# Samples' value products with probabilities stationary, and their last chain inside the cz tiles

## What is computed

```python
o_cmp, p_cmp = cmp_attention(q, pos, kc, vc)                # 63 compressed keys
o_slc = slc_attention(q_rot, pos, idx, ks_blk, vs_blk)      # 1024 cached keys + the new one
o_win = win_attention_cached(q_rot, pos, ...)               # window of 512
g3 = jax.nn.sigmoid(cg).reshape(B, T, 3, C_HEADS, 1)
oc = g3[:, :, 0] * o_cmp + g3[:, :, 1] * o_slc + g3[:, :, 2] * o_win
yc = oc.reshape(B, T, C_WIDTH).astype(x.dtype) * jax.nn.silu(cz)
```

## Time and profile before

| what | us |
|---|---|
| median of 3 runs (lowest to highest) | 1960.08 (1957.07 to 1964.10) |
| the profiled execution | 1959.96 |
| its span | 1958.2 |
| TensorE matmuls busy | 1695.2 (87%) |
| DVE, ACT, POOL busy | 955.0, 560.5, 481.6 |
| mean granted TensorE clock | 0.918 |

### The profile page before, as it was taken

One profiled execution on the slowest core, in us unless ns is written; L12 is line 12 of the kernel. 1 busy time (PEld: TensorE's weight loads), 2 busy tenths in 40 slices (PEclk: granted clock), 3 DMA queues, 4 the chain that ended last, 5 costly groups with the idle time before them and its releaser, 6 DMA issues. The chain is left out here.

```text
span 1958.2 us, 30111 instructions
## 1 busy us (share of the span) xinstructions
PE 1695.2 (87%) x11721; PEld 1503.9 (77%) x11721; DVE 955.0 (49%) x1621; ACT 560.5 (29%) x1111; POOL 481.6 (25%) x468
## 2 busy tenths in 40 slices
PE   7899978988886999999896996978778996999797
PEld 3789965666665888888796986878677985899797
DVE  0651466666640222422212394858454265568676
ACT  0312125444431232332110342434232355100100
POOL 2022101000011111111202472737363212124400
PEclk9999959999988999999897997979789997999899
DMA  8401140000005444343303110202021201344422
GB/s 297 139 11 45 23 99 1 1 2 2 1 21 146 117 114 109 103 112 100 134 22 120 33 33 11 68 15 63 11 88 55 60 23 45 139 143 141 153 77 76
DMA packets 166720, 144.47 MB, mean 74 GB/s; under 512 B 55254, under 2 KB 156594, under 8 KB 165682
## 3 DMA queue, kind: packets, MB, share of 16 engines
q1 hardware_dynamic: 157586, 128.80, 22.0%
q10 hardware_dynamic: 8992, 13.74, 2.0%
HBM read 117.32 MB, written 29.40 MB: 75 GB/s over the span
## 5 line engine op out<-in xcount | busy, mean ns | idle before, releaser
L1008 PE MATMUL ps<-w_hi,h_hi 128*128 128x256 f32 x792 | 229.8, 290 | 19.1 <-DVE h_lo L2462 13.6
L1008 PE MATMUL ps<-h_hi,w_hi 128*128 128x344 f32 x648 | 222.8, 344 | 10.0 <-DVE aq L2301 5.1
L1008 PE MATMUL ps<-w_lo,h_hi 128*128 128x256 f32 x792 | 225.4, 285 | 0.0
L1008 PE MATMUL ps<-w_hi,h_lo 128*128 128x256 f32 x792 | 225.3, 284 | 0.0
L1008 PE MATMUL ps<-h_lo,w_hi 128*128 128x344 f32 x648 | 216.2, 334 | 0.0
L1008 PE MATMUL ps<-h_hi,w_lo 128*128 128x344 f32 x648 | 215.2, 332 | 0.0
L1008 PEld LDWEIGHTS ps<-w_hi,h_hi 128*128 128x128 f32 x792 | 152.7, 193 | 20.2 <-issue 14.5
L1008 PE MATMUL ps<-h_hi,wg_hi 128*128 128x344 f32 x432 | 148.5, 344 | 14.9 <-ACT gate_stage L1752 13.7
L890 POOL CAST w_hi<-w_raw 128x1024 fp32r<-128x1024 f32 (+1 forms) x50 | 53.7, 1074 | 419.2 <-DMA w_raw<-in_w_in 186.6
L1008 PEld LDWEIGHTS ps<-w_lo,h_hi 128*128 128x128 f32 x792 | 152.7, 193 | 0.0
L1008 PEld LDWEIGHTS ps<-w_hi,h_lo 128*128 128x128 f32 x792 | 152.6, 193 | 0.0
(11 more groups left out here) (434 smaller groups left out, 3620.6 us busy)
## 6 DMA issues: line engine op xcount, KB each, us to landing
w_raw<-in_w_in SPq DMA_DIRECT2D x46, 512.0 KB, 5.1
sgm<-gate_spill SPq DMA_DIRECT2D x22, 516.0 KB, 5.7
gate_spill<-gate_stage ACTq DMA_DIRECT2D x54, 172.0 KB, 2.5
w_raw<-in_w_in SPq DMA_DIRECT2D x34, 256.0 KB, 3.4
adw<-in_ada_w SPq DMA_DIRECT2D x8, 1024.0 KB, 11.2
pgc<-in_cache_nsa_kv SPq DMA_DIRECT2D x128, 64.0 KB, 2.4
pg<-in_cache_nsa_kv SPq DMA_DIRECT2D x64, 128.0 KB
w_raw<-in_w_branch SPq DMA_DIRECT2D x12, 512.0 KB, 4.5
```

Of the source, the lines that this page charges most:

```text
L1008: last = mm(out, lhsT=l, rhs=r, start=(i == 0 and j == 0), stop=(i == n - 1 and j == 2))
```

## The change

The value products exchange their operands: 8 columns of `PTS` are stationary and 128 columns of values move, so that the outputs come as 8 rows (heads) x 384. DVE copies them to the dead rows of `CS` or `CSR` (`OT8`), and SP places each sample's 8 rows by a DMA in rows `8b` to `8b + 7` of a new tile `OROW` (`o_rows`), for samples 0 to 5 in front of the value loads of the sample two later, for sample 6 behind the last sample's loads, and for sample 7 behind the loads of cz's weights. DVE waits for the placement before it writes the same buffer again. The transposes of `OTS` (L1407) and `OTS` itself are gone. The spreading of the cz and gate rows stands behind tile 4 of cz, DVE's chain behind tile 5 (with ACT's two sigmoids), and the turning back behind tile 7; the copy into `YF` and `yc_done` stay behind the last tile.

```diff
@@ -405,12 +405,13 @@
     QBD = sb("qbd", o_, [2, 64]); o_ += 128
     NKT = sb("nkt", o_, [8]); o_ += 8
     PTS = sb("pts", o_, [112]); o_ += 112
-    OTS = sb("ots", o_, [3, 64]); o_ += 192
     SM8 = sb("sm8", o_, [16], parts=8); o_ += 16
     assert o_ <= END
     o_ = O_F + 14864
     PW8 = sb("pw8", o_, [512], parts=8); o_ += 512
     NVR = sb("nvr", o_, [2, P], parts=1); o_ += 256
+    OROW = sb("o_rows", o_, [3, P], parts=64); o_ += 384
+    OT8 = [CS[:, 0:384], CSR[:, 0:384]]
     assert o_ <= O_F + 16128
     EXQ = sb("exq", O_SRW, [512], parts=64)
     QROW = sb("qrow", O_SRW + 512, [2, P], parts=64)
@@ -505,6 +506,7 @@
     gate_full, gate_free = sem("gate_full"), sem("gate_free")
     gate_out = [sem("gate_out%d" % i) for i in range(2)]
     spilled = sem("spilled")
+    o_placed, placed_before = [ld["x2"], adw_in[3]], 5 * 16
     half_split = sem("half_split")
     w_used = sem("w_used")
     own = {n: sem("own_" + n) for n in ("act", "dve", "pool")}
@@ -714,6 +716,12 @@
         sp.wait_ge(outs, total[0])
         cache = a["cache_nsa_kv"][0].rearrange("n p f g d -> n p (f g d)")
         npool = cache.shape[0]
+
+        def place_output(b):
+
+            sp.wait_ge(e("s_ots"), b + 1)
+            sp.dma_start(OROW[8 * b:8 * b + 8].rearrange("q x c -> q (x c)"), OT8[b % 2]).then_inc(o_placed[b % 2], 16)
+
         for b in range(NS):
             def page(j):
                 i = sp.value_load(KP[0:1, 8 * b + j:8 * b + j + 1], min_val=0, max_val=npool - 1)
@@ -736,6 +744,7 @@
             load_more_gate_weights(2 * b + 3 + (b >= 3))
             if b >= 2:
                 sp.wait_ge(e("s_pv"), b - 1)
+                place_output(b - 2)
             for j in range(8):
                 sp.dma_start(PG[:, b % 2, j, :], page(j).rearrange("o p c -> p (o c)")[:, 256:512]).then_inc(pg_in[b % 2], 16)
             wv = swin[b].rearrange("(t p) c -> p t c", p=P)
@@ -743,11 +752,13 @@
             sp.dma_start(WR[:, b % 2, 1:4, :], wv[:, 1:4, :]).then_inc(pg_in[b % 2], 16)
             sp.dma_start(WR[0:1, b % 2, 0, :], CS[b:b + 1, 1024:1280]).then_inc(pg_in[b % 2], 16)
             sp.dma_start(NVR[:, b % 2, :], CS[b:b + 1, 896:1024]).then_inc(pg_in[b % 2], 16)
+        place_output(NS - 2)
         load_more_gate_weights(len(SGATES))
         sp.wait_ge(half_split, halves_plain + len(SGATES))
         half[0] += len(SGATES)
         for u in range(U_CZ, U_A):
             load_unit(u)
+        place_output(NS - 1)
         for b in range(NS):
             out_dma(win_s[b, 0:511, :], swin[b, 1:512, :])
         load_unit(U_A)
@@ -1362,12 +1373,12 @@
             nc.tensor.transpose(ps[:, 6, 0:8], PW8[:, 384:512], ID[0:8, 0:8]).then_inc(e("s_pt"), 1)
             gates(b, 8)
             pe.wait_ge(e("s_pts"), b + 1)
-            mm(ps[:, 6, 8:16], lhsT=VCS[0:NCMP, :], rhs=PTS[0:NCMP, 0:8], start=True, stop=True)
+            mm(ps[0:8, 6, 0:P], lhsT=PTS[0:NCMP, 0:8], rhs=VCS[0:NCMP, :], start=True, stop=True)
             for i in range(8):
-                mm(ps[:, 6, 16:24], lhsT=PG[:, s, i, P:2 * P], rhs=PTS[:, 8 + 8 * i:16 + 8 * i], start=(i == 0), stop=False)
-            mm(ps[:, 6, 16:24], lhsT=NVR[:, s, :], rhs=PTS[0:1, 72:80], start=False, stop=True)
+                mm(ps[0:8, 6, P:2 * P], lhsT=PTS[:, 8 + 8 * i:16 + 8 * i], rhs=PG[:, s, i, P:2 * P], start=(i == 0), stop=False)
+            mm(ps[0:8, 6, P:2 * P], lhsT=PTS[0:1, 72:80], rhs=NVR[:, s, :], start=False, stop=True)
             for i in range(4):
-                last = mm(ps[:, 6, 24:32], lhsT=WR[:, s, i, P:2 * P], rhs=PTS[:, 80 + 8 * i:88 + 8 * i], start=(i == 0), stop=(i == 3))
+                last = mm(ps[0:8, 6, 2 * P:3 * P], lhsT=PTS[:, 80 + 8 * i:88 + 8 * i], rhs=WR[:, s, i, P:2 * P], start=(i == 0), stop=(i == 3))
             last.then_inc(e("s_pv"), 1)
             gates(b, 9)
         pe.wait_ge(e("s_ots"), NS)
@@ -1396,20 +1407,19 @@
             last.then_inc(pz.full, 1)
             if t >= 2:
                 yc_transposes(pe, t - 1)
+            if t == 4:
+                pe.wait_ge(e("cs_cz"), 1)
+                mm(ps[0:64, 6, 0:512], lhsT=G[0:8, GE8:GE8 + 64], rhs=CS[:, 1304:1816], start=True, stop=True)
+                mm(ps[0:64, 7, 0:24], lhsT=G[0:8, GE8:GE8 + 64], rhs=CS[:, 1280:1304], start=True, stop=True).then_inc(e("f_psum"), 1)
+            if t == 7:
+                pe.wait_ge(e("f_sbuf"), 2)
+                for i in range(4):
+                    last = mm(ps[:, 7, 416 + 8 * i:424 + 8 * i], lhsT=YSM[:, P * i:P * i + P], rhs=G[0:64, GE64:GE64 + 8], start=True, stop=True)
+                last.then_inc(e("f_psum"), 1)
         pe.wait_ge(pz.full, 9)
         pe.sem_inc(w_used, 2)
         yc_transposes(pe, 8)
 
-        pe.wait_ge(e("cs_cz"), 1)
-        mm(ps[0:64, 6, 0:512], lhsT=G[0:8, GE8:GE8 + 64], rhs=CS[:, 1304:1816], start=True, stop=True)
-        mm(ps[0:64, 7, 0:24], lhsT=G[0:8, GE8:GE8 + 64], rhs=CS[:, 1280:1304], start=True, stop=True)
-        for i in range(3):
-            last = nc.tensor.transpose(ps[0:64, 7, 32 + P * i:32 + P * i + P], OTS[:, i, :], ID)
-        last.then_inc(e("f_psum"), 1)
-        pe.wait_ge(e("f_sbuf"), 2)
-        for i in range(4):
-            last = mm(ps[:, 7, 416 + 8 * i:424 + 8 * i], lhsT=YSM[:, P * i:P * i + P], rhs=G[0:64, GE64:GE64 + 8], start=True, stop=True)
-        last.then_inc(e("f_psum"), 1)
         pe.wait_ge(e("yc_done"), 1)
 
 
@@ -1810,11 +1820,12 @@
                 st(A(SGZ[:, t % 2, :], ps[:, t % 4, :], ACT.Sigmoid), e("z_sig"))
             if t >= 2:
                 yc_out(act, st, t - 1)
+            if t == 5:
+                act.wait_ge(e("f_psum"), 1)
+                st(A(CGX, ps[0:64, 7, 0:24], ACT.Sigmoid), e("f_sig"))
+                act.wait_ge(e("f_sbuf"), 1)
+                st(A(CZ2, CZ1, ACT.Sigmoid), e("f_sig"))
         yc_out(act, st, 8)
-        act.wait_ge(e("f_psum"), 1)
-        st(A(CGX, ps[0:64, 7, 0:24], ACT.Sigmoid), e("f_sig"))
-        act.wait_ge(e("f_sbuf"), 1)
-        st(A(CZ2, CZ1, ACT.Sigmoid), e("f_sig"))
 
         def a_group(h, i):
             S = AS[h % 2]
@@ -2246,7 +2257,33 @@
             st(cp(PTS[:, 80:104], ps[:, 7, 484:508]))
             st(cp(PTS[:, 104:112], ps[:, 6, 0:8]), e("s_pts"))
             v.wait_ge(e("s_pv"), b + 1)
-            st(cp(OTS[:, :, 8 * b:8 * b + 8], ps[:, 6, 8:32].rearrange("p (x h) -> p x h", x=3)), e("s_ots"))
+            if b >= 2:
+                v.wait_ge(o_placed[b % 2], placed_before + 16 * (b // 2))
+            st(cp(OT8[b % 2], ps[0:8, 6, 0:384]), e("s_ots"))
+
+        hm = G[0:64, GHM:GHM + 8]
+
+        def sample_rows():
+
+            v.wait_ge(e("f_psum"), 1)
+            st(tt(CZX.rearrange("p (h d) -> p h d", d=HD), ps[0:64, 6, :].rearrange("p (h d) -> p h d", d=HD), bc(hm.unsqueeze(2), [64, 8, HD]), MUL))
+            st(V.reduce_sum(CZ1, CZX.rearrange("p (h d) -> p d h", d=HD), AX), e("f_sbuf"))
+            for x in range(2):
+                v.wait_ge(o_placed[x], placed_before + 16 * NS // 2)
+            for i in range(3):
+                st(ts(OSB[:, i, :], OROW[:, i, 0:HD], G[0:64, GGM:GGM + 1], None, MUL))
+                st(stt(OSB[:, i, :], in0=OROW[:, i, HD:P], scalar=G[0:64, GGM + 1:GGM + 2], in1=OSB[:, i, :], op0=MUL, op1=ADD))
+            v.wait_ge(e("f_sig"), 1)
+            cg = CGX.rearrange("p (x h) -> p x h", x=3)
+            st(tt(cg, cg, bc(hm.unsqueeze(1), [64, 3, 8]), MUL))
+            st(V.reduce_sum(GX, cg, AX))
+            st(ts(OSB[:, 0, :], OSB[:, 0, :], GX[:, 0:1], None, MUL))
+            for i in (1, 2):
+                st(stt(OSB[:, 0, :], in0=OSB[:, i, :], scalar=GX[:, i:i + 1], in1=OSB[:, 0, :], op0=MUL, op1=ADD))
+            v.wait_ge(e("f_sig"), 2)
+            st(tt(CZ1, CZ1, CZ2, MUL))
+            st(tt(CZ1, CZ1, OSB[:, 0, :], MUL))
+            st(tt(YSM.rearrange("p (h d) -> p h d", d=HD), bc(CZ1.unsqueeze(1), [64, 8, HD]), bc(hm.unsqueeze(2), [64, 8, HD]), MUL), e("f_sbuf"))
 
         v.wait_ge(e("cs_cz"), 1)
         st.mark(pz.free)
@@ -2257,25 +2294,8 @@
             st(tt(YTK[:, (t - 1) % 2, :], SGZ[:, t % 2, :], ps[:, t % 4, :], MUL), pz.free)
             y3 = YTK[:, (t - 1) % 2, :].rearrange("p (a c) -> p a c", a=4)
             st(tt(y3, y3, QT[:, :, P * (t - 1):P * t], MUL), e("yc_tok"))
-        v.wait_ge(e("f_psum"), 1)
-        hm = G[0:64, GHM:GHM + 8]
-        st(tt(CZX.rearrange("p (h d) -> p h d", d=HD), ps[0:64, 6, :].rearrange("p (h d) -> p h d", d=HD), bc(hm.unsqueeze(2), [64, 8, HD]), MUL))
-        st(V.reduce_sum(CZ1, CZX.rearrange("p (h d) -> p d h", d=HD), AX), e("f_sbuf"))
-        v.wait_ge(e("f_sig"), 1)
-        for i in range(3):
-            st(ts(OSB[:, i, :], ps[0:64, 7, 32 + P * i:32 + P * i + 64], G[0:64, GGM:GGM + 1], None, MUL))
-            st(stt(OSB[:, i, :], in0=ps[0:64, 7, 96 + P * i:160 + P * i], scalar=G[0:64, GGM + 1:GGM + 2], in1=OSB[:, i, :], op0=MUL, op1=ADD))
-        v.wait_ge(e("f_sig"), 1)
-        cg = CGX.rearrange("p (x h) -> p x h", x=3)
```

(11 more changed lines are left out.)

## The result

The changed kernel takes **1936.0 us** (median of 4 runs, 1933.48 to 1942.34), the kernel before 1961.19 in runs beside it (4 runs, 1957.07 to 1964.1). The ratio is 0.987, 95% interval 0.9842 to 0.9899: 25.2 us less between the medians. The forecast was 1933.7, between 1925 and 1953. Two later sets of runs on other chips gave 0.9879 (0.9853 to 0.9905) and 0.9862 (0.9837 to 0.9888).

What follows compares the result with a forecast made beforehand. TensorE, busy 87% of the span, was taken as the bound, with its clock and the tail after cz telling most. 1960.0 - 18.5 + 0.4 + 2.0 - 10.35 = 1933.6, 1933.7 against the median; range 1925 to 1953.

Steps and rivals of the forecast that it cites:

- rival A: The author's own forecast, all terms as summed: 1933.7 us, its own range 1925 to 1942; chance 0.70.
- Step 1: Sample stage, value matmuls with operands exchanged: 28 instructions a sample, 0.107 to 0.12 us apart; no change in time.
- Step 2: Sample stage: the seven falls of TensorE's clock beside value groups go; 18.5 us gained, bounds 0 and 20.4.
- Step 3: DVE's wider copy of the outputs: covered for samples 0 to 6, TensorE waits for the last before cz; +0.4 us.
- Rival B: Clock falls stay, following from something near the groups or few array columns in use; 1952 us; chance 0.14.
- Step 4: Eight small DMAs on SP: about 0.34 us an issue, loads about 1 us later, covered by SP's waits; cost 0.
- Step 5: cz stage: work moved in costs TensorE 2.0 us (1.5 to 3.0); tile 6's products 1.5 us late, cost 0.
- Step 6: Tail after cz: spill 10.35 us earlier, head's third group still follows const_a; bounds 9.0 and 13.4 us.

Runs made afterwards that it cites:

- the kernel with the values alone: The changed kernel with the samples' last chain put back behind the cz tiles; 1948.05 us, ratio 0.9923 to the kernel before.
- the kernel with the other order of products: The changed kernel with const_a loaded early, spill in two parts, ACT's first sigmoid before the casts, tile 8's two products swapped; 1936.47 us, ratio 0.9864.

## Why the prediction was right

The forecast was 1933.7 with rival A at 0.70; the median was 1936.0. By its own steps:

**Step 1, operands exchanged, 0.** Right. 28 instructions, the 16 of the pages 1.92 us where the old ones took 1.95, about 0.12 us each.

**Step 2, the clock, -18.5.** Right in cause and size. All seven falls are gone from the profiled execution. From the first group to cz TensorE's busy time is 16.2 us less (298.6 and 282.4; the stage is 15.6 shorter, since its idle time grew by 0.6, 0.35 of that being step 3). The part of the fall at 979.5 that lay in the cz stage gave 2.6 more: from cz's first matmul to the last tile's first transposes it was 61.7 us, and it is 59.1 in the kernel with the values alone. That makes 18.8. That the matmuls' form is what lowers the clock at samples 0 to 6, and not something near the groups, is shown by the pair of kernels with 14 extra matmuls, one form of which brings falls back and the other not. The prediction said that it isn't idle time that goes before these falls, and for the last sample that isn't so: a wait of 1.2 us stands just ahead of its group and one of 4.8 us some 8 us earlier, and a shorter fall comes there in four of ten traces with the new form. The form made that fall longer (6.8 to 10.2 us in the three kernels with the old form alone, 3.4 or none in the new), but it isn't the only cause. Rival B had the falls follow from the small transposes or from the few columns in use; with both in place the clock stays at 1.00. The Trainium skill's page "TensorE: Matmul & The Clock Gate" ("Why this matters for your kernels") has the clock go with idle gaps between matmuls. That holds for part of what is seen here: each of the six falls between the groups with fourfold placement opened in a wait or just behind it, and those waits are 26.6 us together. It doesn't cover groups without a gap ahead of them: those of samples 0 to 6 had 33.9 us at half clock before the change.

**Step 3, the copy, +0.4.** Right: 0.546 us where 0.182 stood, and TensorE's wait for it ahead of cz is 0.7 us.

**Step 4, eight placements at no cost.** Right for this kernel but for 1.1 us, and by an argument that doesn't hold. An issue took 0.82 us, not the 0.34 that I took from the spill's row. The page loads went out 0.8 us after the end of a group before the change (716.15) and go out 2.9 us after it now (716.49 behind 713.62), so they are 2.1 us later and not 1. SP's waits shrank from 10.8 to 8.1 us a sample, where I had "some 7", and from these I concluded that nobody waits. With four placements SP's waits hardly shrank further, and TensorE lost 34 us in the stage. What the term needed was the distance from the end of a value group to the landing of NVR, against TensorE's time over the same stretch, and I read only the queue's waits. The rows for it, NVR's load for sample 3 and TensorE's first matmul behind it, before and after (sample 1's group ends at 715.40 and at 713.62):

```profile
728.24 0.58 SPq L745 DMA_DIRECT2D nvr<-cs  x1
738.54 1.04 PE L1289 MATMUL ps<-const_g,pg 128*128 128x128 f32 x8
```
```profile
729.31 0.52 SPq L754 DMA_DIRECT2D nvr<-cs  x1
735.39 1.09 PE L1300 MATMUL ps<-const_g,pg 128*128 128x128 f32 x8 [0.89 <-DMA nvr<-cs]
```

From the end of the group it was 12.8 us to the load and 23.1 to TensorE; now it is 15.7 and 21.8, the wait included. The load takes 6.1 us until TensorE may start, so 4.2 us had been to spare. The later issue took 2.8 of them and the quicker TensorE 2.3, and the 0.9 that is missing is the wait. The new waits of 0.89 and 0.23 us were not foreseen.

**Step 5, the cz stage, +2.0.** The stage is 0.1 us shorter as measured; with the 2.6 us of the fall that is counted in step 2 put back it is 2.5 longer. The kernel with the values alone, which has neither the fall nor the work put in, shows the same, 59.1 us where the kernel after has 61.6. DVE's lateness for tile 6 was 1.4 us (1.5 foreseen) and cost TensorE nothing.

**Step 6, the tail, -10.35.** Right: 10.3 from the last transposes to the spill, and the third group of the head followed const_a, 14.4 us behind the spill as before. TensorE's wait there was 2.8 us where I had said about 4, because its first two groups ran longer at half clock, until 1036.2, 6.9 us behind the spill, where it had been 3.4:

```profile
1026.00:1036.20 10.20, 6.74 (x24) 6.37 (x25) 1.30 (x2) 0.60 (x1) 7.69 (x5) 0.50 0.79 266
```

That fall opens at the wait for tile 8's product. The chain's being taken away didn't remove it, and it doesn't show in the sum since const_a was the later of the two.

The profiled executions are 26.5 us apart, and the steps sum to 26.4. So close an agreement is in part luck, since 1.2 us of it comes from behind the third group, where the code is the same, and 0.7 went the other way at 647. The medians, 25.2 apart, are the better measure.

## What to carry to other kernels

Where TensorE is busy throughout and its granted clock still dips, lay the dips beside the shapes of the matmuls: a run of them that loads 128 columns to stream 8 cost this kernel half its clock for 3.4 to 6.8 us at most of its samples, and exchanging the operands, at the price of a wider copy and a small DMA, took it away at seven of eight samples and shortened or removed it at the last, which follows a wait. A queue's wait is not slack: before putting work on it, measure from the event that releases it to the landing of the last load behind it, and compare with when the consumer wants that. When the last chain of a stage is taken off the path, look for what was loaded or split just behind it. Here const_a loaded earlier, with the spill in two parts and ACT's wait moved (the three were not tried singly), was worth another 3 us by its place and 5 to 6 between the medians.

## What was not expected

- **Products of DVE and POOL over SBUF held one another up, and the first one won.** DVE's product of two SBUF operands takes 0.69 us alone and 2.67 beside POOL's TENSOR_TENSOR of 2.34 us; when DVE came first it took 0.76 to 0.97 and POOL's took 2.67. The sum is about what it would be one after the other. A product with one operand in PSUM was not held: it took its 0.69 us in the middle of POOL's (1027.74 in the kernel with the other order of products). A small TENSOR_SCALAR reading SBUF was held too, 2.01 us for 0.25, until POOL's operation ended at 1034.36. The Trainium skill ("SBUF — State Buffer", "SBUF: two separate sides") has it that a DVE instruction with two SBUF inputs contends with a GpSimd instruction that reads SBUF, and that whichever starts first has the shared ports for its whole instruction while the other blocks fully; the product's rows agree with that. Why the TENSOR_SCALAR was held is not shown by a run of its own.
- **A placement from SBUF to SBUF holds SP 0.82 us** where the spill's issue takes 0.34, with 8 partitions of 1.5 KB. Repeated at once it is 0.63 us, and it lands 1.2 us after SP begins to wait for it.
- **Interleaving helps only in part.** Narrow matmuls alternated with ones of 344 streamed columns left 27.2 of 40.7 us of falls, with one at a sample that had had none.
